# Block inversions issued inside the next turn's dense tile, in a two-layer hybrid decoder step

## What is computed

```python
h  = mod1(pre1(x));  P = h @ w_in
yA = RWKV-7 time mixing;  yB = gated DeltaNet (chunked)
L = where(strict, einsum(k_beta, kb) * decay, 0)
tinv = triangular_solve(eye + L, eye)          # one for each chunk and head
u = tinv @ v_beta;  w = tinv @ (k_beta * exp(gc))
x += gate1 * post1((sigmoid(gA) * yA + sigmoid(gB) * yB) @ w_out)
```

## Time and profile before

| | us |
|---|---|
| median of 3 runs | 2051.51 (2046.51 to 2052.93) |
| the profiled execution | 2044.36 |
| its span | 2042.6 |
| mean granted clock of TensorE | 0.961 |

### The profile page before, as it was taken

How to read it: one execution, slowest core, us unless ns; L and a number is a source line. 1 busy time by engine, 2 the same in 40 slices (tenths; PEclk the granted TensorE clock), 3 DMA queues, 4 the chain that set the end, 5 groups by cost and what they waited for, 6 DMA issues and landing times.

```text
span 2042.6 us, 45362 instructions
## 1 busy us (share of the span) xinstructions
PE 1912.5 (94%) x19380; PEld 1741.4 (85%) x19380; DVE 1253.3 (61%) x2158; ACT 939.6 (46%) x1834; POOL 65.3 (3%) x138
## 2 busy tenths in 40 slices
PE   6999989989999998899999999899999999789998
PEld 4899978888888877788989999788899788679997
DVE  3555356766446667678556654578654566769963
ACT  3334465444456524433444444645444764253343
POOL 0000000110000100000000000000200010000000
PEclk7999999989999988999999999999899998899999
DMA  7877755546464564699775666545543436269873
GB/s 254 239 224 221 206 173 169 168 130 166 118 177 133 151 166 111 192 285 273 204 209 149 181 176 186 165 135 156 136 125 94 137 102 161 65 163 254 255 201 108
DMA packets 556070, 353.37 MB, mean 173 GB/s; under 512 B 19428, under 2 KB 515078, under 8 KB 554318
## 3 DMA queue, kind: packets, MB, share of 16 engines
q1 hardware_dynamic: 490634, 302.74, 52.1%
q10 hardware_dynamic: 61396, 43.01, 8.1%
q0 software_dynamic: 3840, 4.73, 0.9%
HBM read 332.27 MB, written 18.50 MB: 172 GB/s over the span
## 4 chain that ended last, share of the span: by engine, by line
PE 74%; DVE 9%; DMA 8%; ACT 5%; issue 2%; POOL 1%; ACTq 1%; SPq 0%; DVEq 0%; POOLq 0%
PE bank L907 71%; DMA ring<-in_ffn_up 3%; DMA ring<-in_w_ada 2%; DVE ring_r L741 2%; PE bank L654 1%; DMA far<-t_blocks 1%; ACT w_hi_r L733 1%; DMA far<-in_state_gdn_ssm 1%; DVE far L1967 1%; PE bank L667 1%; POOL far L635 1%; DVE y L1967 1%; DVE big L1967 1%; PE bank L662 1%; DVE big L1970 1%
## 5 line engine op out<-in xcount | busy, mean ns | idle before, releaser
L907 PE MATMUL bank<-big_r,w_hi_r 128*128 128x264 f32 x4160 | 1078.4, 293 | 43.8 <-DVE h_r L1970 25.2
L907 PE MATMUL bank<-big_r,ring_r 128*128 128x264 f32 (+1 forms) x3456 | 995.0, 288 | 0.0
L907 PEld LDWEIGHTS bank<-big_r,w_hi_r 128*128 128x128 f32 x4160 | 749.1, 191 | 106.6 <-issue 86.2
L907 PE MATMUL bank<-h_r,w_hi_r 128*128 128x264 f32 x2752 | 797.6, 290 | 0.0
L741 DVE TENSOR_TENSOR ring_r<-ring,w_hi_r 128x1024 fp32r<-128x1024 f32 (+2 forms) x440 | 523.7, 1195 | 393.1 <-ACT w_hi_r L733 389.3
L907 PEld LDWEIGHTS bank<-big_r,ring_r 128*128 128x128 f32 (+1 forms) x3456 | 663.4, 192 | 1.0
L733 ACT CAST w_hi_r<-ring 128x1024 fp32r<-128x1024 f32 (+2 forms) x440 | 452.1, 1028 | 447.8 <-PE bank L907 199.4
L907 PEld LDWEIGHTS bank<-h_r,w_hi_r 128*128 128x128 f32 x2752 | 531.0, 193 | 1.6 <-issue 0.5
L907 PE MATMUL bank<-ring,c 128*32 128x256 f32 x1152 | 95.3, 413 | 15.1 <-DMA ring<-in_w_ada 12.4
L907 PE MATMUL bank<-big,far 64*64 64x64 f32 (+2 forms) x1440 | 103.6, 255 | 0.0
L907 PEld LDWEIGHTS bank<-big,far 64*64 64x64 f32 (+1 forms) x1440 | 87.0, 139 | 7.1 <-issue 6.6
(11 more groups left out here) (301 smaller groups left out, 1931.0 us busy)
## 6 DMA issues: line engine op xcount, KB each, us to landing
ring<-in_ffn_up SPq DMA_DIRECT2D x176, 512.0 KB, 4.9
ring<-in_w_in SPq DMA_DIRECT2D x148, 512.0 KB, 3.7
ring<-in_w_ada SPq DMA_DIRECT2D x144, 512.0 KB, 4.3
ring<-in_ffn_down SPq DMA_DIRECT2D x64, 512.0 KB, 4.3
far<-in_state_gdn_ssm ACTq DMA_DIRECT2D x28, 512.0 KB, 5.8
ring<-in_ffn_down SPq DMA_DIRECT2D x32, 384.0 KB, 3.5
ring<-in_w_out SPq DMA_DIRECT2D x16, 512.0 KB, 4.3
out_sample_gdn_ssm<-far ACTq DMA_DIRECT2D x16, 512.0 KB, 5.2
```

Of the source, the lines that this page charges most:

```text
L907: return pe.matmul(out, lhsT, rhs, start=start, stop=stop)
```

## The change

The steps of a lot are issued one turn later and inside that turn's dense tile: `linear` calls `invert` before slice 2 and before slice 6 of 8. Steps 0, 2 and 3 are cut in two halves of 8 units; step 1 is cut by kind, its L662 matmuls in the first place and its L667 matmuls in the second. Step s of a lot is thus in `dense(INV0[run] + s + 1)`. Step 3 of lots 1 and 2 stays behind the dense tile of its turn (41 and 75), because the reader of the result follows. VectorE's, ScalarE's and GpSimd's programs are as before, and so are all semaphore counts.

```diff
-        def invert(pe, run, s):
+        def invert(pe, run, s, part_of):
 
             lt, both, x_b = inv_sets[run]
             n = 4 + s // 2
-            if s == 0:
+            own = range(UNITS // 2 * part_of, UNITS // 2 * (part_of + 1)) if s != 1 else range(UNITS)
+            if part_of == 0 and s == 0:
 
                 pe.wait_ge(block_out.sem, block_out.at(9 * (run + 1)))
...
-            elif s == 2:
+            elif part_of == 0 and s == 2:
                 pe.wait_ge(inv_t.sem, inv_t.at(2 * run + 1))
             if s % 2 == 0:
-                for u in range(UNITS):
+                for u in own:
...
-                i.then_inc(inv_pe.sem, inv_pe.one())
+                if part_of:
+                    i.then_inc(inv_pe.sem, inv_pe.one())
                 return
-            pe.wait_ge(inv_x.sem, inv_x.at(2 * run + s // 2 + 1))
-            if n < 5:
-                for u in range(UNITS):
+            if part_of == 0:
+                pe.wait_ge(inv_x.sem, inv_x.at(2 * run + s // 2 + 1))
+            if n < 5 and part_of == 0:
+                for u in own:
...
                 i.then_inc(inv_pe.sem, inv_pe.one())
-            for u in range(UNITS):
+                return
+            for u in own:
...
-            i.then_inc(inv_pe.sem, inv_pe.one())
+            if part_of:
+                i.then_inc(inv_pe.sem, inv_pe.one())
...
                         for k in range(kt):
                             if k == kt // 2 and pair is not None:
                                 products(pair)
+                            if step is not None and k in (kt // 4, kt // 2 + kt // 4):
+                                invert(pe, *step, k // (kt // 2))
...
-                        linear(banks[k % 2][0:tile_size(*TILES[k])[1], 0:T], TILES[k], hi_in, h_lo, pair=pair)
+                        step = None
+                        for run in range(3):
+                            if 0 <= t - 1 - INV0[run] < (4, 3, 3)[run]:
+                                step = run, t - 1 - INV0[run]
+                        linear(banks[k % 2][0:tile_size(*TILES[k])[1], 0:T], TILES[k], hi_in, h_lo, pair=pair, step=step)
...
-                        for run in range(3):
-                            if 0 <= t - INV0[run] < 4:
-                                invert(pe, run, t - INV0[run])
+                        for run in (1, 2):
+                            if t - INV0[run] == 3:
+                                invert(pe, run, 3, 0)
+                                invert(pe, run, 3, 1)
```

More of the change, by code:

```diff
@@ L915, in weights, with linear @@
                                 ring_r[:, slot[n], 0:kt * cols].rearrange("p (k n) -> p k n", k=kt))
-                    def linear(out, key, x_hi, x_lo, start=True, stop=True, pair=None):
+                    def linear(out, key, x_hi, x_lo, start=True, stop=True, pair=None, step=None):
                         hi, lo = weights((l, *key))
```

## The result

The changed kernel took 2058.86 us (median of 20 executions, 2045.62 to 2067.42) against 2051.81 us for the kernel before in the same runs: a ratio of 1.0036, 95% interval 1.0022 to 1.005. It is 0.36% slower. The forecast was "no difference that can be seen", 2050.2 us by a sum of -1.3 us, and about +7 us came. The time lies above the forecast's own range of 2045 to 2056 us and only just under 2059, the outer limit. The profiled execution took 2059.07 us with a span of 2057.3 and a mean granted clock of 0.961.

A forecast was written before the change was run, and what follows sets the result against it. TensorE, busy 94% of the span, was taken as the bound, worst in the lots' waits and half clock. Terms -5.0 + 0.9 - 0.4 + 0.2 + 1.5 + 1.5 = -1.3 us gave 2050.2 us, range 2045 to 2056.

The forecast's parts named there:

- Lot 2, layer 0: From lot 2's landing to the first matmul behind it: shorter wait, clock staying up, 5.0 us less.
- Lot 2, layer 1: Same stretch in layer 1: no wait to shorten, clock full, 0.9 us more.
- the sentence under which I said the forecast would be wrong: Sign: forecast wrong if the clock falls inside lots that have no long wait, or stays up through all.
- Borders: Entering and leaving small matmuls inside dense tiles: 0.25 us a step, between 0.09 and 0.4; 3.0 us in all.
- When lot 1's blocks land: Landing of lot 1's blocks behind lot 0's end: taken 1.5 us later in each layer, called the doubtful term.
- the late end: Bad end for lot 1's landing: half clock in lot 0 as before, landing 3.8 us later, 2.7 in layer 1.
- The clock stays up: Rival: 2.4 GHz kept in lot 0 and in lot 1 of both layers; -11.8 us, 2039.7 us; chance 0.22.
- VectorE held inside the dense tiles: Rival: lot 0's half clock stays, `dense(36)` waits, lot 1 lands later; +3.9 to +7.3 us, 2055.4 to 2058.8; chance 0.2.

The follow-up runs named there:

- e12: The kernel before with only layer 0's ada piece of turn 72 moved to turn 44: ratio 0.9985 to the kernel before.
- e9: The kernel before with only lot 2 moved into the dense tiles, each step whole at the middle: ratio 1.0 to the kernel before.
- e16: All lots moved, lots 0 and 1 whole, lot 2 cut, ada piece of turn 72 in turn 44: ratio 0.9981 to the kernel before.
- e6: All lots moved with each step whole at the tile's middle, ada piece of turn 72 in turn 44: ratio 0.992 to the kernel before.
- e5: The changed kernel with layer 0's ada piece of turn 72, and its load, moved to turn 44: ratio 1.0 to the kernel before.
- e15: All lots moved, lots 0 and 1 cut, lot 2 whole, ada piece of turn 72 in turn 44: ratio 0.9964 to the kernel before.
- e4: The changed kernel with each step whole at the middle of the tile, in all lots: ratio 0.9953 to the kernel before.
- e3: The kernel before with only lot 0 moved into the dense tiles, steps cut: ratio 0.9985 to the kernel before.
- e7: The kernel before with only lots 0 and 1 moved, each step whole at the middle: ratio 0.9968 to the kernel before.
- e1: The kernel before with only lots 0 and 1 moved into the dense tiles, steps cut: ratio 0.9966 to the kernel before.
- e11: The changed kernel with the ada piece of turn 72 in turn 44 and TensorE's samples(6) in turn 72: ratio 0.9992 to the kernel before.
- e13: All lots moved, steps whole, ada piece of turn 72 in turn 44, samples(6) in turn 72: ratio 0.9918 to the kernel before.

## Why the prediction was wrong

The forecast failed in lot 2: -4.1 us for both layers, where e2, which moves lot 2 alone, measured +6.5 us in the means (2060.9 against 2054.4). Two steps of it failed, one in each layer.

*Lot 2, layer 0 (taken -5.0, measured +5.5 in the profile).* The first step that failed: "the ada piece (0.6) and a quarter of `dense(73)` (0.73) are done before the landing, the wait falls from 2.56 to about 1.2 us". I counted the piece as work that can be done then, and did not look when its weight tile lands. Its tile landed at 698.93; the piece waited 3.65 us, longer than the wait that was to be halved, and the clock fell 0.8 us behind its start. The row of before that would have told it is the issue at 695.81 with the use at 703.57: whoever takes 4.7 us (7.76 less 3.05) of cover from in front of the use has to ask what the DMA then has. The runs price its removal at 0.3%, of which up to 0.15% may not be the wait's (e12).

*Lot 2, layer 1 (taken +0.9, measured +8.7).* The second step that failed, and by the runs the larger one: "Clock full" was read from one profile of an unmoved lot. The cut steps lose clock without any wait: 6 to 7 us a kernel for the six steps of lot 2, by three pairs of kernels (e2 less e9, e16 less e6, e5 less e15) and by the profiles. That was the sentence under which I said the forecast would be wrong. The Trainium skill ("TensorE: Matmul & The Clock Gate", "HAM oscillation — how this bites in real kernels") explains lost clock by waits for data; the wait for the piece and the gain in lots 0 and 1 agree with it, the 17.07 us at half clock with 17.07 us busy do not. Nearer to these comes its next section ("A second HAM failure mode: psum-queue depth-cycling"), in which, for bf16 matmuls that cycle through PSUM banks, very short idle times between groups of matmuls are enough. The borders of a cut step would be such places, but the ends of matmuls are modelled in the records, so no row here shows an idle time there.

*Borders (taken 0.25 us a step, bounds 0.09 to 0.4; 3.0 us in all, since lot 0's were put at nothing, under a VectorE wait).* The mechanism was right and the term too small: 0.31 us a cut in the timeline, 0.35 and 0.4 from the rest of e5 less e6 and of the change less e4 (6.9 and 8.1 us over 20 steps). Lot 0's are not hidden: in e3 the rest grows by 4.9 us for its eight steps. The whole term is the cut's; moved whole, a step costs nothing that shows in the rest.

*When lot 1's blocks land (taken +1.5 a layer).* Right in its place, wrong in the value. `dense(36)` was held by VectorE until 461.00 (460.8 forecast). The clearing, from ScalarE's timeline,
```profile
466.57 1.92 ACT L624 ACTIVATE far<-ident 128x2048 f32<-128x2048 f32 x1 [2.69 <-DVE far L699]
```
ended at 468.5 (468.0 to 472.6 forecast). The clock stayed up through the waits of 2.02 and 1.04 us, so the late end never came. The scatter landed some 8 us behind the clearing rather than 9.7, since its last DMA took 3.70 us to land and not 5.49. No run shows why; for the forecast it was luck. So TensorE waited 0.95 us for lot 1's blocks in layer 0 and 0.61 in layer 1, where some 3.1 and 2.4 were forecast. From step 0 of lot 0 to step 0 of lot 1 it is 35.5 us against 37.7 before in layer 0, and 35.2 against 35.6 in layer 1.

*The rivals.* "The clock stays up" came true for lots 0 and 1: 24 of 35 us at half clock are gone in whatever form the steps are moved, 8 to 11 us of time in e7 and e1. It had a chance of 0.22, and lot 1's clock was priced at -6.5 us in it. "VectorE held inside the dense tiles" did not come: its condition, a half clock in step 1 of lot 0, was not met in layer 0 of the changed kernel's profile. Its 2055.4 to 2058.8 us is the time that came, but by chance: the other side was reached by two mechanisms that were no rival of mine, the piece's wait and the clock lost by the cut. The means of all executions split the result so: lots 0 and 1 moved whole -9.3 us (e7: -0.9 rest, -8.4 clock); lot 2 moved whole, with its new wait, about 0 (e4 less e7, +0.3); the cut +12.9 us (the change less e4: 8.1 rest, 4.8 clock). They add up to +3.9 us across groups of runs. Within the change's own group the means differ by 5.8 us and the ratio says 0.36%, 7.4 us, so 2 to 3 us are the error of comparing groups.

*What stays open.* Why a cut costs clock in lot 2 and none that shows in lots 0 and 1. Lot 2's turns also hold `samples(6)`, tiny matmuls in front of step 1, but moving them out did not show (e11 against e5, e13 against e6). No kernel tried other cuts of lot 2 or single steps of it, so which of its three cut steps lets the clock go was not found. Nor are the cut and the place told apart: a whole step stands at the middle, the parts at a quarter and three quarters, and no kernel has a whole step elsewhere.

## What to carry to other kernels

When work is moved out from in front of an instruction, list what that instruction and its neighbours load, and compare issue, landing and new use: the cover lost may be a DMA's. Put small matmuls between dense ones in one piece rather than in several: each cut cost here 0.3 us and, in one lot of three, another microsecond of clock. Where the clock falls by chance, compare the clock loss and the rest over many executions, and not two profiles.

## What was not expected of the hardware

- The granted clock fell with TensorE busy throughout: 17.07 us at 0.50 in 1710.12 to 1727.19, amid alternating dense tiles and blocks of 32 to 64 matmuls of 64 x 64 by 32 columns in fp32; the same matmuls with each step in one piece were at 0.50 for 3.4 us at most over both layers' lots 2, in five profiles.
- It did not fall behind waits of 2.02, 1.04 and 0.95 us in lots 0 and 1 of layer 0, where it had fallen behind 3.31 and 2.79 us. This is not strict: in the profile of e5_ada72 it fell for 10.24 us at 440.73, beside a wait of 1.83 us in the same place.
- A load of 512 KB for the conditioning product took 6.66 us from issue to landing while the scatter into the cleared buffer was under way, against a median of 4.4 us (3.4 to 11.6) for the 144 such loads of the kernel. That the scatter is the reason was not tested.
